# Two token tiles in turn, matmul by matmul, in the products whose tokens are stationary

## The chip, the cores and the metric

The kernel runs on one core of one Trainium2 chip. The metric is the device time of one execution in microseconds (us), as the median of several runs; lower is better. The profile comes from one further execution, so its own length is given beside the median.

## What is computed

The reference is one layer (DEPTH = 1) of a hybrid backbone, all in float32. 256 context tokens and 256 latent tokens of width 2048 are modulated and go through one input projection. The latent tokens then pass three branches (a gated recurrence, a pooling mixer, windowed attention), whose outputs are merged and projected, and a squared-ReLU MLP follows:

```python
ul = (xl * (1 + sc1_l) + sh1_l) @ w_in
uc = (xc * (1 + sc1_c) + sh1_c) @ w_in
...
z = jnp.einsum('btjc,jcd->btjd', jnp.stack(ys, axis=2), w_branch)
gates = jax.nn.sigmoid(u[..., COL_GATE:].reshape(B, T, N_BRANCH, D_MODEL))
return jnp.sum(gates * z, axis=2) @ w_out
...
xl = _layer_norm(ALPHA * xl + g1_l * _merge_branches(...), ln1_g, ln1_b)
h = xl * (1 + sc2_l) + sh2_l
xl = _layer_norm(ALPHA * xl + g2_l * (jnp.square(jax.nn.relu(h @ w_ff1)) @ w_ff2), ln2_g, ln2_b)
```

The four products that the change touches are those with the gate columns of `w_in`, with `w_branch`, with `w_out` and with `w_ff2` (2048 x 2048 four times over, since D_FF is 8192).

## The kernel before

**Precision.** Every float32 weight and activation is split into a rounded part and the rest (`whi`, `wlo`; index 0 and 1 of `hCL`, `yR`, `mR`, `hid`). A product is three matmuls: x high with w high, x high with w low, x low with w high.

**Weights.** A panel is 512 rows by 512 columns and is read by one DMA into a ring of `raw` buffers. It is split in two halves of 256 rows each: the ACT engine casts the half into `whi` (L476, semaphore `hi_made`), and DVE subtracts to get `wlo` (L940, semaphore `lo_made`). There are four places for halves, so ACT may cast a half only once the PE has finished with the half four before it (`w_used`, or `blk_done` for the last half of a block). In the order of both engines the splits stand between their other work, at places written out by hand.

**Products with the tokens stationary** (`tokens`, L1468 to L1470). The output block is 256 tokens by 512 columns: two token tiles t of 128, each in a PSUM bank of its own (`main[:, banks + t]`). The stationary operand is a 128 x 128 piece of the tokens, the moving one a 128 x 512 row tile of the weights. A half holds two row tiles j. For a half the PE does tile 0 whole (two j by three matmuls, six into one bank), then tile 1 (six into the other bank): 12 matmuls. The last matmul of tile 0 in the block raises `blk_done` and the last of tile 1 raises it again; the reader of tile 0 waits for the first, the reader of tile 1 for the second. `bank` waits, ahead of a tile's first matmul, until the bank's earlier reader has released it (`freed_by_act`, `freed_by_dve`).

**Blocks of this kind.** For each branch j of three and each of four column groups pp: a gate block of four panels in banks 0 and 1, read by ACT with a sigmoid (`sg`, L654), and a branch block of two panels in banks 2 and 3, read by DVE (`m_t` L1154, `gz` L1160). In between stand attention steps of the PE (L1730, L1740, L1751). Then four blocks with `w_out` (`out`), read by DVE in `out_rows`: L1230, L1233 and the statistics L1235 for tile 0, the same for tile 1. Then the MLP in four rounds f; each has four blocks of `wide` (L1445, L1447, features stationary against `h2`) and four blocks i of `tokens` against `hid`, read by DVE in `ff_out`: for f = 0 a copy (L1286), for f = 1 and 2 an add (L1288), for f = 3 three operations for each tile (L1291, L1293, L1295). In the last block of `out` and the last block of all, `apart=4` keeps the two tiles apart: tile 0 runs through all panels, then tile 1.

**What stands behind a reader.** DVE executes in order. In the round f = 3 its list is, between two blocks: `ff_out` for both tiles, then `residual` (L1324, L1326), then the split of the next panel (L940 twice). In `out` it is `out_rows` for both tiles, then splits.

Of the kernel before, what the change touches and what calls it, by code (L numbers as in the profile page):

```python
# [30 lines left out]
TILES = (slice(0, P), slice(P, T))  # L31
# [137 lines left out]
ST = stream()  # L169
# [80 lines left out]
def build(nc, vecs, cst, rcnt, masks, xT, xtok, rows, w_ad1, w_ada, w_in, w_ck, w_cv, pool_w, w_br, w_out, w_f1, w_f2, outT):  # L250
    weights_of = {"w_ad1": w_ad1, "w_ada": w_ada, "w_in": w_in, "w_ck": w_ck, "w_cv": w_cv, "w_br": w_br, "w_out": w_out,
                  "w_f1": w_f1, "w_f2": w_f2}
    with ExitStack() as ctx:
# [24 lines left out]
        def half_at(q):  # L278

            if q >= HALVES - 4 or OUT3 <= q < OUT3 + 4:  # L280
                return whi_end[:, q % 4], wlo_end[:, q % 4]
            if MLP0 <= q < MLP0 + 2:
                return whi_top[:, q - MLP0], wlo_top[:, q - MLP0]
            n = (q if q < MLP0 else q - 2) % 4
            return whi[:, n], wlo[:, n]
# [98 lines left out]
        main = ctx.enter_context(nc.psum_tensor("main", [P, 4, 512], F32))  # L384
# [10 lines left out]
        w_used, blk_done = ended["w_used"], ended["blk_done"]  # L395
# [975 lines left out]
        def _(pe):  # L1371
            mm = nc.tensor.matmul

            def bank(name, first, b):
                need = PN.before[name, first][b]
                if need:
                    pe.wait_ge(freed[need[0]], need[1])

            def half_ready(name, n, h):
                q = ST.half(name, n, h)  # L1380
                pe.wait_ge(lo_made, q + 1)
                return q % 4
# [72 lines left out]
            def tokens(name, first, chunks, banks, x, ready=None, between=lambda k: None, apart=0, second=None):  # L1455


                def half(n, h, t):
                    half_ready(name, first + n, h)
                    w_hi, w_lo = half_at(ST.half(name, first + n, h))  # L1460
                    if n == 0 and h == 0:
                        bank(name, first, t)
                    for j in range(2):
                        kt = 4 * n + 2 * h + j
                        start, stop = kt == 0, kt == 4 * chunks - 1
                        own = slice(P * t, P * (t + 1))
                        out = main[:, banks + t]
                        mm(out, x[:, kt, 0, own], w_hi[:, j], start=start, stop=False)  # L1468
                        mm(out, x[:, kt, 0, own], w_lo[:, j], start=False, stop=False)  # L1469
                        last = mm(out, x[:, kt, 1, own], w_hi[:, j], start=False, stop=stop)  # L1470
                    end = n == chunks - 1 and h == 1
                    if end:
                        last.then_inc(blk_done, 1)
                    elif t == 1:
                        last.then_inc(w_used, 1)

                for n in range(chunks - apart):
                    if ready is not None:
                        ready(n)
                    for h in range(2):  # L1480
                        for t in range(2):
                            half(n, h, t)
                    between(n)
                for t in range(2):
                    for n in range(chunks - apart, chunks):
                        if ready is not None and t == 0:
                            ready(n)
                        if second is not None and t == 1:
                            second(n)
                        for h in range(2):  # L1490
                            half(n, h, t)
# [109 lines left out]
            for n in range(2):  # L1601
                for h in range(2):
                    par = half_ready("cv", n, h)
                    w_hi, w_lo = (w[:, par].rearrange("p a (c n) -> p (a c) n", c=2) for w in (whi, wlo))
                    for b in range(2):
                        if n == 0 and h == 0:
                            bank("cv", 0, b)
                        for j in range(4):
                            kt = 8 * n + 4 * h + j
                            x, start, stop = (hC, hL)[b], kt == 0, kt == KT - 1  # L1610
                            for tile in range(2):
# [5 lines left out]
                                last = mm(out, x[:, kt, 1, own], w_hi[:, j], start=False, stop=stop,  # L1617
                                          skip_group_check=tile == 1)
# [22 lines left out]
            for it in range(4):  # L1641
                def between(k):
                    if k == 0:
                        if it:
                            ada_turn(3 + it)
                        if it >= 2:
                            keys_turned(it - 2)
                    if k == 1 and it >= 2:
                        states(it - 2)
# [62 lines left out]
            def branch(j, pp, between):  # L1712
                first = 24 * j + 6 * pp
                tokens("gates", first, 4, 0, hL, between=between)
                tokens("gates", first + 4, 2, 2, yR[j % 2], ready=lambda k: pe.wait_ge(y_lo, j + 1),
                       between=lambda k: between(4 + k))
# [41 lines left out]
            for b in range(8):  # L1758
# [5 lines left out]
                for n in range(2):  # L1764
                    last = mm(out, pw_sb[:, b // 2 * 2 + n, P * (b % 2):P * (b % 2 + 1)], pd[:, b // 2 * 2 + n],
                              start=n == 0, stop=n == 1)
# [53 lines left out]
            for i in range(4):  # L1820
                tokens("out", 4 * i, 4, 2 * (i % 2), mR, ready=lambda k: pe.wait_ge(m_lo, k + 1),
                       between=lambda k: merged(3) if i == 0 and k == 0 else None, apart=4 if i == 3 else 0,
                       second=first_rows)
# [111 lines left out]
```

## Time and profile before

| | us |
|---|---|
| median of three runs | 1905.89 (1905.32 to 1906.68) |
| span of the profiled execution | 1903.2 |
| stretch with gate and branch blocks | 631.2 to 1074.6 |
| blocks with `w_out` | 1074.6 to 1162.4 |
| `tokens` blocks of the MLP, rounds 0 to 3 | from 1264.0, 1442.5, 1620.9 and 1799.3 |

The median stands 2.7 us over the span of the profiled execution. In the profile PE is the matmul engine and PEld its weight load, which overlaps; a matmul's recorded duration (0.39 us) is longer than the distance to the next one's start (0.23 us), since the matmuls overlap in the pipeline, so distances between starts are what is to be read. An entry in brackets says how long the engine had been idle and what ended it.

### The profile page before, as it was taken

The numbers are of one execution on the slowest core, as the hardware profiler recorded it, in microseconds if no ns is written. First come the engines' busy times: TensorE is split into PE (matmuls) and PEld (weight loads), VectorE is DVE, ScalarE is ACT, GpSimd is POOL, SyncE is SP. The second block draws the span as 40 slices with busy tenths as digits, with TensorE's granted clock in tenths as the row PEclk, the third lists the DMA queues.
The fourth block names the chain that finished last, engine by engine and source line by source line (L and its number), as shares of the span: only waits on it lengthen the run. The fifth ranks groups of instructions, "written<-read, shape, count | busy, mean of one in ns | idle before, by whom it ended". The sixth has DMA issues, their size and how long they took to land.

```text
span 1903.2 us, 24662 instructions
## 1 busy us (share of the span) xinstructions
PE 1860.8 (98%) x10072; PEld 1568.8 (82%) x10072; DVE 1287.1 (68%) x1470; ACT 816.7 (43%) x991; POOL 282.8 (15%) x165
## 2 busy tenths in 40 slices
PE   6999999999999999999999998999999999999997
PEld 3678888899999877877888887888888888888875
DVE  2246777776969676577767667876676567557786
ACT  2132234464555554444444445443344344434432
POOL 0000000005757262001001000110012001100200
PEclk9999999999999999999999999999999999999998
DMA  9967765553434454565776763665665556556652
GB/s 398 418 251 280 267 224 195 177 178 133 155 112 155 158 185 155 190 252 199 272 258 227 281 218 136 237 228 199 252 234 203 195 203 242 207 188 241 223 177 89
DMA packets 60176, 408.93 MB, mean 215 GB/s; under 512 B 6432, under 2 KB 9120, under 8 KB 11936
## 3 DMA queue, kind: packets, MB, share of 16 engines
q1 hardware_dynamic: 55584, 395.34, 57.2%
q10 hardware_dynamic: 4480, 12.02, 1.7%
q8 instruction: 80, 1.31, 0.3%
q14 instruction: 32, 0.26, 0.0%
HBM read 405.24 MB, written 2.10 MB: 214 GB/s over the span
## 4 chain that ended last, share of the span: by engine, by line
PE 90%; DVE 4%; DMA 2%; DVEq 2%; ACT 1%; POOL 1%; issue 0%; SPq 0%; ACTq 0%
PE main L1468 14%; PE main L1470 14%; PE main L1469 14%; PE side L1445 6%; PE main L1445 6%; PE main L1385 5%; PE main L1387 5%; PE main L1386 5%; PE side L1447 3%; PE main L1447 3%; DMA raw<-in_w_ad 2%; PE main L1522 2%; PE main L1523 1%; PE main L1524 1%; PE side L1502 1%; DVE wlo L940 1%
## 5 line engine op out<-in xcount | busy, mean ns | idle before, releaser
L940 DVE TENSOR_TENSOR wlo<-raw,whi 128x1024 fp32r<-128x1024 f32 x542 | 696.6, 1312 | 307.1 <-ACT whi L476 306.3
L476 ACT CAST whi<-raw 128x1024 fp32r<-128x1024 f32 x542 | 563.9, 1050 | 715.0 <-PE main L1470 394.4
L1385 PE MATMUL main<-hCL,whi 128*128 128x256 f32 (+1 forms) x768 | 247.7, 323 | 0.9 <-DVE wlo L940 0.9
L1387 PE MATMUL main<-hCL,wlo 128*128 128x256 f32 (+1 forms) x768 | 244.5, 318 | 0.0
L1386 PE MATMUL main<-hCL,whi 128*128 128x256 f32 (+1 forms) x768 | 244.4, 318 | 0.0
L961 DVE SCALAR_TENSOR_TENSOR asum<-raw,sm,asum 128x512 f32<-128x512 f32 x240 | 221.8, 924 | 19.5 <-issue 0.4
L1468 PE MATMUL main<-whi,hid 128*128 128x512 f32 x496 | 194.9, 393 | 2.5 <-DVE wlo L940 2.5
L1469 PE MATMUL main<-wlo,hid 128*128 128x512 f32 x496 | 193.1, 389 | 0.0
L1470 PE MATMUL main<-whi,hid 128*128 128x512 f32 x496 | 193.0, 389 | 0.0
L1445 PE MATMUL side<-h,whi 128*128 128x512 f32 x512 | 181.3, 399 | 0.0
L1445 PE MATMUL main<-h,whi 128*128 128x512 f32 x480 | 170.0, 399 | 2.4 <-DVE wlo L940 2.4
L1468 PE MATMUL main<-whi,hCL 128*128 128x512 f32 x384 | 156.0, 406 | 0.0
L1385 PEld LDWEIGHTS main<-hCL,whi 128*128 128x128 f32 x768 | 146.2, 190 | 11.4 <-DVE wlo L940 1.3
L1386 PEld LDWEIGHTS main<-hCL,whi 128*128 128x128 f32 x768 | 146.2, 190 | 10.1 <-issue 0.2
L1387 PEld LDWEIGHTS main<-hCL,wlo 128*128 128x128 f32 x768 | 146.1, 190 | 10.1
L1470 PE MATMUL main<-whi,hCL 128*128 128x512 f32 x384 | 149.8, 390 | 0.0
L1469 PE MATMUL main<-wlo,hCL 128*128 128x512 f32 x384 | 149.7, 390 | 0.0
L1447 PE MATMUL side<-h,wlo 128*128 128x256 f32 x512 | 143.8, 281 | 0.0
L1447 PE MATMUL main<-h,wlo 128*128 128x256 f32 x496 | 138.6, 281 | 0.0
L925 POOL TENSOR_TENSOR sq<-sq 128x1024 f32<-128x1024 f32 x16 | 31.6, 1975 | 656.4 <-ACT hid L776 656.4
L1445 PEld LDWEIGHTS side<-h,whi 128*128 128x128 f32 x512 | 96.2, 188 | 24.1
L1468 PEld LDWEIGHTS main<-whi,hid 128*128 128x128 f32 x496 | 93.1, 188 | 24.0 <-issue 4.6
(264 smaller groups left out, 2920.5 us busy)
## 6 DMA issues: line engine op xcount, KB each, us to landing
raw<-in_w_f SPq DMA_DIRECT2D x128, 1024.0 KB, 4.8
raw<-in_w_in SPq DMA_DIRECT2D x104, 1024.0 KB, 4.8
raw<-in_w_ada SPq DMA_DIRECT2D x64, 1024.0 KB, 4.9
raw<-in_w_ad SPq DMA_DIRECT2D x32, 1024.0 KB, 16.1
raw<-in_w_br SPq DMA_DIRECT2D x24, 1024.0 KB, 4.9
raw<-in_w_out SPq DMA_DIRECT2D x16, 1024.0 KB, 4.8
xin<-in_xT SPq DMA_DIRECT2D x8, 512.0 KB, 17.4
raw<-in_w_ck SPq DMA_DIRECT2D x4, 512.0 KB, 15.1
```

The lines of the kernel that those rows point to most:

```text
L476: nc.scalar.copy(half_at(q)[0], slots[slot][:, 2 * h:2 * h + 2]).then_inc(hi_made, 1)
L940: TT(half_at(q)[1], slots[slot][:, 2 * h:2 * h + 2], half_at(q)[0].bitcast(F32), ALU.subtract).then_inc(lo_made, 1)
L961: last = STT(asum[:], slots[slot][:, j], s, asum[:], ALU.mult, ALU.add)
L1385: mm(out, w_hi, x_hi, start=start, stop=False)
L1386: mm(out, w_hi, x_lo, start=False, stop=False)
L1387: return mm(out, w_lo, x_hi, start=False, stop=stop)
L1445: mm(ps[:, b], w_hi[:, j, own], h2[:, kt].rearrange("p v t -> p (v t)"), start=kt == 0, stop=kt == 15, skip_group_check=True)
L1447: last = mm(ps[:, b, 0:T], w_lo[:, j, own], h2[:, kt, 0], start=False, stop=kt == 15, skip_group_check=True)
L1468: mm(out, x[:, kt, 0, own], w_hi[:, j], start=start, stop=False)
L1469: mm(out, x[:, kt, 0, own], w_lo[:, j], start=False, stop=False)
L1470: last = mm(out, x[:, kt, 1, own], w_hi[:, j], start=False, stop=stop)
L1522: mm(main[:, b], x[:, kt, 0, tile], whi[:, par, j], start=kt == 0, stop=False)
```

## The change

In the blocks that are not kept apart, a new function `both` takes the place of two calls of `half`. It issues the same 12 matmuls of a half in another order: for each row tile j it does x high with w high for tile 0 and then tile 1, x high with w low for both, and x low with w high for both. Neighbouring matmuls then write different banks, read the same moving weights, and have different stationary pieces. Each bank still gets its matmuls in the same order. Both banks are waited for ahead of the block's first matmul, and the wait for the half stands once instead of twice. `blk_done` is raised by the last matmul of tile 0, which is now the last but one of the block, and by the last of tile 1. The two blocks with `apart=4` still use `half`.

```diff
+                def both(n, h):
+                    half_ready(name, first + n, h)
+                    w_hi, w_lo = half_at(ST.half(name, first + n, h))
+                    if n == 0 and h == 0:
+                        bank(name, first, 0)
+                        bank(name, first, 1)
+                    for j in range(2):
+                        kt = 4 * n + 2 * h + j
+                        start, stop = kt == 0, kt == 4 * chunks - 1
+                        for t in range(2):
+                            mm(main[:, banks + t], x[:, kt, 0, TILES[t]], w_hi[:, j], start=start, stop=False)
+                        for t in range(2):
+                            mm(main[:, banks + t], x[:, kt, 0, TILES[t]], w_lo[:, j], start=False, stop=False)
+                        for t in range(2):
+                            last = mm(main[:, banks + t], x[:, kt, 1, TILES[t]], w_hi[:, j], start=False, stop=stop)
+                            if stop:
+                                last.then_inc(blk_done, 1)
+                    if n < chunks - 1 or h == 0:
+                        last.then_inc(w_used, 1)
+
                 for n in range(chunks - apart):
                     if ready is not None:
                         ready(n)
                     for h in range(2):
-                        for t in range(2):
-                            half(n, h, t)
+                        both(n, h)
                     between(n)
```

The order on the PE at the end of the block f = 3, i = 0, before: its last half and the first matmul of the next block. The first six matmuls are tile 0, the next six tile 1; the names don't show the bank.

```order
L1468 MATMUL main<-whi,hid 128x512 [waits lo_made]
L1469 MATMUL main<-wlo,hid 128x512
L1470 MATMUL main<-whi,hid 128x512
L1468 MATMUL main<-whi,hid 128x512
L1469 MATMUL main<-wlo,hid 128x512
L1470 MATMUL main<-whi,hid 128x512
L1468 MATMUL main<-whi,hid 128x512 [waits lo_made]
L1469 MATMUL main<-wlo,hid 128x512
L1470 MATMUL main<-whi,hid 128x512
L1468 MATMUL main<-whi,hid 128x512
L1469 MATMUL main<-wlo,hid 128x512
L1470 MATMUL main<-whi,hid 128x512
```

The same half after the change (L1487, L1489 and L1491 are the three lines of `both`; x2 is a pair, tile 0 and then tile 1):

```order
L1487 MATMUL main<-whi,hid 128x512 [waits lo_made]
L1487 MATMUL main<-whi,hid 128x512
L1489 MATMUL main<-wlo,hid 128x512 x2
L1491 MATMUL main<-whi,hid 128x512 x2
L1487 MATMUL main<-whi,hid 128x512 x2
L1489 MATMUL main<-wlo,hid 128x512 x2
L1491 MATMUL main<-whi,hid 128x512 x2
```

The last matmul of tile 0 stood sixth of the twelve and now stands eleventh; that of tile 1 is the twelfth both times.

The start of the second `w_out` block on the PE, before:

```order
L1468 MATMUL main<-whi,mR 128x512 [waits freed_by_dve,lo_made,m_lo]
L1469 MATMUL main<-wlo,mR 128x512
L1470 MATMUL main<-whi,mR 128x512
L1468 MATMUL main<-whi,mR 128x512
L1469 MATMUL main<-wlo,mR 128x512
L1470 MATMUL main<-whi,mR 128x512
L1468 MATMUL main<-whi,mR 128x512 [waits freed_by_dve,lo_made]
```

and after:

```order
L1487 MATMUL main<-whi,mR 128x512 [waits freed_by_dve,lo_made,m_lo]
L1487 MATMUL main<-whi,mR 128x512
L1489 MATMUL main<-wlo,mR 128x512 x2
L1491 MATMUL main<-whi,mR 128x512 x2
```

The wait for the second bank, which stood ahead of the seventh matmul, has joined the one ahead of the first. The lists of ACT, DVE, POOL and SP are the same before and after, and the PE has as many matmuls, 9468.

## Rows read from the trace of the kernel before

**Rows 1.** The page: busy us and share, and the chain that ended last.
```profile
PE 1860.8 (98%) x10072; PEld 1568.8 (82%) x10072; DVE 1287.1 (68%) x1470; ACT 816.7 (43%) x991; POOL 282.8 (15%) x165
...
PE 90%; DVE 4%; DMA 2%; DVEq 2%; ACT 1%; POOL 1%; issue 0%; SPq 0%; ACTq 0%
```

**Rows 2.** Stretches: start:end, length, busy us of each engine, clock, DMA.
```profile
1074.60:1162.40 87.80, 87.80 (x397) 72.86 (x396) 55.68 (x61) 38.17 (x46) 3.04 (x2) 1.00 0.58 213
...
1799.30:1893.00 93.70, 88.89 (x388) 72.02 (x386) 73.28 (x84) 32.55 (x36) 4.63 (x2) 1.00 0.41 139
```

**Rows 3.** Timeline of PE in `out`: start us, duration us, engine, line; second and third block.
```profile
1097.23 0.39 PE L1468 MATMUL main<-whi,mR 128*128 128x512 f32 x1
...
1098.36 0.39 PE L1470 MATMUL main<-whi,mR 128*128 128x512 f32 x1
1098.59 0.39 PE L1468 MATMUL main<-whi,mR 128*128 128x512 f32 x1
1098.81 0.39 PE L1469 MATMUL main<-wlo,mR 128*128 128x512 f32 x1
...
1102.67 0.39 PE L1468 MATMUL main<-whi,mR 128*128 128x512 f32 x1
...
1118.99 0.39 PE L1468 MATMUL main<-whi,mR 128*128 128x512 f32 x1
```

**Rows 4.** Line L1468 and tile `hid`: weight loads, count, ns min/median/max.
```profile
L1468 PEld LDWEIGHTS main<-whi,hid x496: 186/188/188, 1263.9 to 1884.2; 128*128 128x128 f32 x166
L1469 PEld LDWEIGHTS main<-wlo,hid x496: 187/188/189, 1264.1 to 1884.4; 128*128 128x128 f32 x166
```

**Rows 5.** Timeline of DVE in round 0: the readers of tiles 0 and 1.
```profile
1350.86 0.69 DVE L1286 COPY acc<-main 128x512 f32<-128x512 f32 x1 [1.77 <-PE main L1470]
1352.22 0.69 DVE L1286 COPY acc<-main 128x512 f32<-128x512 f32 x1 [0.67 <-PE main L1470]
```

**Rows 6.** Timeline of DVE in round 3, between blocks i = 0 and 1.
```profile
1820.82 0.69 DVE L1291 TENSOR_TENSOR res<-main,g2b 128x512 f32<-128x512 f32 x1 [1.76 <-PE main L1470]
...
1822.97 0.67 DVE L1291 TENSOR_TENSOR res<-main,g2b 128x512 f32<-128x512 f32 x1
...
1826.65 2.36 DVE L940 TENSOR_TENSOR wlo<-raw,whi 128x1024 fp32r<-128x1024 f32 x2
```

**Rows 7.** Timeline of PE in round 3: the three matmuls that waited.
```profile
1828.02 0.47 PE L1468 MATMUL main<-whi,hid 128*128 128x512 f32 x1 [0.44 <-DVE wlo L940]
...
1850.47 0.47 PE L1468 MATMUL main<-whi,hid 128*128 128x512 f32 x1 [0.44 <-DVE wlo L940]
...
1871.40 0.47 PE L1468 MATMUL main<-whi,hid 128*128 128x512 f32 x1 [1.62 <-DVE wlo L940]
```

**Rows 8.** Timeline of DVE in `out`, from tile 0's reader to the split.
```profile
1096.07 0.69 DVE L1230 TENSOR_TENSOR res<-main,g1b 128x512 f32<-128x512 f32 x1 [1.77 <-PE main L1470]
...
1100.37 4.81 DVE L940 TENSOR_TENSOR wlo<-raw,whi 128x1024 fp32r<-128x1024 f32 x4
1106.72 1.23 DVE L940 TENSOR_TENSOR wlo<-raw,whi 128x1024 fp32r<-128x1024 f32 x1 [1.54 <-ACT whi L476]
```

**Rows 9.** Timeline of ACT in the gate stretch.
```profile
729.81 0.60 ACT L654 ACTIVATE sg<-main 128x512 f32<-128x512 f32 x1 [3.94 <-PE main L1470]
731.17 0.60 ACT L654 ACTIVATE sg<-main 128x512 f32<-128x512 f32 x1 [0.76 <-PE main L1470]
...
737.08 1.05 ACT L476 CAST whi<-raw 128x1024 fp32r<-128x1024 f32 x1 [1.14 <-PE main L1470]
```

**Rows 10.** Timeline of PE at the start of a `wide` block and of the next.
```profile
1553.03 0.40 PE L1445 MATMUL side<-h,whi 128*128 128x512 f32 x1
1553.27 0.28 PE L1447 MATMUL side<-h,wlo 128*128 128x256 f32 x1
...
1575.64 0.40 PE L1445 MATMUL main<-h,whi 128*128 128x512 f32 x1
```

**Rows 11.** Timeline of PE: 256 columns each; an early stop.
```profile
560.02 0.28 PE L1386 MATMUL main<-hCL,whi 128*128 128x256 f32 x1
560.14 0.28 PE L1387 MATMUL main<-hCL,wlo 128*128 128x256 f32 x1
...
44.46 0.85 PE L1502 MATMUL side<-raw,sR 128*32 128x256 f32 x12 [2.14 <-DMA raw<-in_w_ad]
```

## The prediction

> **What bounds the kernel now.** I read the page first. The PE is busy 98% of the span and carries 90% of the chain that ended last [rows 1]. The table by stretches says where that is not quite so: in `out` the PE is busy all of 87.80 us, in round 3 of the MLP only 88.89 of 93.70, with the clock at 1.00 in both [rows 2]. So two things can move the time: the distance from one matmul to the next, and the few places where the PE waits. The timeline of the PE gives the distance, and the waits on `wlo` name DVE as the engine behind the places [rows 7].
>
> **Distance between matmuls.** The second `w_out` block starts at 1097.23 and the third at 1118.99, with 96 matmuls between: 21.76 / 96 = 0.2267 us each [rows 3]. The matmul at 1098.59 is the first of tile 1 and writes another bank than the one at 1098.36: 0.23 us. The next, at 1098.81, stays in its bank and keeps its stationary piece: 0.22 us. So the kernel before already holds the transition that the change multiplies, and it costs the same as the others, to the rounding of a row. `both` issues 3 x 1216 = 3648 matmuls less the 2 x 96 of the blocks kept apart, 3456. The value that I take for the alternation is 0 per matmul. The bounds: the 10 ns of rounding, one way, would be 35 us, but a block of 96 contains 16 switches of bank at 0.2267 on average, so a switch that saved or cost even 5 ns would need the other matmuls to make up for it.
>
> The stationary piece is loaded anew for every matmul, also where it is the one just used: L1468 and L1469 share it, and each has 496 loads of 188 ns [rows 4]. At 188 ns they fit under 227, so separating the two gives no load more and exposes none.
> The Trainium skill (TensorE: Matmul & The Clock Gate, Step-by-step: what each phase is for) says that the stationary operand is loaded once and used for many matmuls, which would speak against parting the pair; here each matmul has a load of its own, so by the trace there is nothing to lose. Were the second load of each of the 1152 pairs saved today, its roughly 107 ns (an estimate by the same page's section LDWEIGHTS, columns / 1.2) would add 123 us if uncovered.
>
> **Waits taken out.** The wait on `lo_made` stands once for each half instead of twice, and the second one never ended anything: by the time tile 1 starts, tile 0 has used the same half. 0. The wait for the second bank moves six matmuls, 1.36 us, earlier. Each bank's last reader is then long done: in `out` banks 0/1 and 2/3 take turns, so the reader of block i has 21.8 us before block i + 2 wants its banks, and the other blocks have at least the 10.9 us of a branch block. 0; if the cover were gone it would be up to 1.36 us for each block.
>
> **Tile 0's result comes later.** Its last matmul moves from sixth to eleventh of twelve: 5 x 0.2267 = 1.13 us. Tile 1's stays. That a reader really follows this moment is seen in round 0, where DVE waits for both tiles: 1350.86 and 1352.22, 1.36 us apart, six matmuls [rows 5]. What this does depends on the length of the reader.
>
> *Short readers* (one operation of 0.6 to 0.7 us): ACT's sigmoid, DVE's `gz`, `m_t`, and `ff_out` in rounds 0 to 2. In round 0 tile 0 would be read at 1350.86 + 1.13 = 1351.99, tile 1 right behind at about 1352.60 instead of 1352.22: what is queued behind, the splits above all, is 0.38 us later. On ACT the sigmoids at 729.81 and 731.17 give 0.3 in the same way, and the engine idles 1.14 us before the cast at 737.08, so it is absorbed there [rows 9]. I take 0 for these; the upper bound is 0.4 us at two or three of the tight attention steps, 1 us in all. A second cost would be a bank that frees late for the `wide` block behind round 0: it wants its third bank four pairs of 0.353 us [rows 10] after 1352.02, at 1353.43, and that bank is read by 1351.99 + 0.69 = 1352.68. Covered.
>
> *Long readers in round 3.* Three operations for tile 0, then three for tile 1: tile 1's first one starts at 1822.97, 2.15 us after tile 0's and without idle time [rows 6]. So nothing of the 1.13 is absorbed: all of DVE's list shifts, through the residual steps to the split at 1826.65. Its first half ends about 1.22 us later, at 1827.87, and the PE has waited for just that and starts at 1828.02 [rows 6, 7]. DVE had come to the reader early (idle 1.76 us), so it follows the PE. Each of the three stops of the PE in round 3 has this form, behind the readers of blocks i = 0, 1 and 2 [rows 7]. The gaps grow from 0.44, 0.44 and 1.62 to 1.57, 1.57 and 2.75: 3 x 1.13 = 3.4 us. Nothing gives it back, since block, reader and end all start from the PE's own time.
>
> *Long readers in `out`.* Same form: reader at 1096.07, no idle time until the splits at 1100.37; the first of them ends at 1100.37 + 1.22 = 1101.59 [rows 8]. The PE takes that half at 1102.67 in step [rows 3], so there is room for 1.08. The least distance of split's end and matmul is 0.15 (1827.87 to 1828.02), so 0.93 is spare and 1.13 - 0.93 = 0.20 us comes out as a new stop. The readers of blocks 0, 1 and 2 do this, and the last of them hits the block kept apart: 3 x 0.20 = 0.6 us.
>
> **Sum.** 0 + 0 + 3.4 + 0.6 = 4.0 us. The profiled execution would span 1903.2 + 4.0 = 1907.2; the median stands 2.7 over that span: 1909.9 us, 0.21% slower.
>
> **Rivals.**
> *The alternation saves time (the other side).* 512 columns take 227 ns and 256 take 120 [rows 11], so by the difference a column is 0.417 ns and every matmul carries 13 ns on top. If this were the price of following in the same bank, all 3456 would save it: 1909.9 - 3456 x 0.0133 = 1864. Against it: a switch of bank shows no saving [rows 3], and it would have to take effect at every switch already there. A saving from 1.2 ns per matmul on (4.0 / 3456) turns the sign.
> The Trainium skill (TensorE: Matmul & The Clock Gate, Back-to-back issue gap) gives N / 2.4 + 2.5 ns, 215.8 for 512 columns, where the row has 227. By that rule, should the alternation reach it, the time would be 37 us less, some 1872; it ties the rest to nothing that this change touches, and the trace does not agree with it.
>
> *The later tile is hidden.* DVE's delay would be absorbed, by the four places for halves. In the gate stretch this holds. In round 3 it fails since the place that the PE waits for is the one behind the reader. If I am wrong there, 1905.9.
>
> *Alternating stationary pieces cost.* In `wide` a pair of 512 and 256 columns takes (1575.64 - 1553.03) / 64 = 353.3 ns [rows 10], where 226.7 + 120 would be 346.7: 3.3 ns a matmul. There every matmul has a new stationary piece. If it is that, and not the short matmul that gives the load little cover, 3456 x 3.3 = 11.4 us come on top: 1921. Against it: in `tokens` two of three matmuls already have a new piece, at 0.2267.
>
> *More comes out of the tight places.* Short readers cost up to 1 us; the pause of 2.75 us is longer than any before with the clock at 1.00 (2.14 [rows 11]). Were the clock to fall to its lower level for the 19 us left, at most those 19 are added; likelier is 1911.5 to 1914.
>
> **Chances and range.** Forecast 0.62 (1908.6 to 1911.5), hidden 0.15 (1905.5 to 1907.5), more from the tight places 0.11, alternating pieces 0.06, saving 0.06. A measurement of this kernel can tell about 0.2%, 3.8 us, from no change; the forecast lies just beyond, at 4.0, so I split it 0.38 slower to 0.24 same. Slower 0.38 + 0.11 + 0.06 = 0.55; same 0.24 + 0.15 = 0.39; faster 0.06. The range 1905.2 to 1913 leaves out the saving, the alternating pieces and the upper part of the tight places, together under 0.2.
>
> **What would show it.** Starts of neighbouring matmuls in `both` 0.2267 apart. Readers of tiles 0 and 1 in round 0 one operation apart, near 0.6, instead of 1.36. The three idle times before a matmul in round 3 near 1.57, 1.57, 2.75, ended by `wlo`. Three new ones of 0.2 in `out`. A distance other than 0.2267 would refute me first; unchanged idle times in round 3 next.

## The result and the profile after the change

| | before | changed |
|---|---|---|
| median, us | 1905.89 (5 runs, 1905.32 to 1906.89) | 1912.5 (5 runs, 1911.55 to 1914.28) |
| ratio, 95% interval | | 1.0033 (1.0022 to 1.0044) |
| span of the profiled execution, us | 1903.2 | 1910.1 |

The change costs time: 6.6 us by the medians of this first comparison, where 4.0 (to 1909.9) were forecast. A second comparison of the same two kernels, further down, gives 1.0022 (1.0013 to 1.0031), about 4.2 us. Both lie past the 0.2% that the prediction set as the bound, the second one barely, and its interval reaches below it. Both profiled pages count 10072 matmuls, before and after; the 9468 named above stands in no view. One of the 11 runs of the first experiment below took 2319.5 us at a granted clock of 0.755, and its ratio is formed without that run.

**The rate of the matmuls has not changed.** Timeline of the PE in the changed kernel: the starts of the second and third blocks of round 0, 96 matmuls apart, and the starts of the second and third `w_out` blocks. `x2` is a pair, tile 0 and tile 1.

```profile
1290.25 0.62 PE L1487 MATMUL main<-whi,hid 128*128 128x512 f32 x2
...
1312.01 0.62 PE L1487 MATMUL main<-whi,hid 128*128 128x512 f32 x2
```

```profile
1098.57 0.62 PE L1487 MATMUL main<-whi,mR 128*128 128x512 f32 x2
1099.02 0.62 PE L1489 MATMUL main<-wlo,mR 128*128 128x512 f32 x2
...
1120.64 0.62 PE L1487 MATMUL main<-whi,mR 128*128 128x512 f32 x2
```

A pair takes 0.45 us from start to start, and the block of round 0 takes 21.76 us for 96 matmuls, 0.2267 for each as in [rows 3] (the `w_out` block is longer, 22.07, by a stop that is told below): no gain from the other bank, none from the shared moving weights, no loss from the changing stationary piece. The loads are as before too, one for each matmul; this is the line of the view by source for the first statement of `both` (compare [rows 4]):

```profile
L1487 PEld LDWEIGHTS main<-whi,hid x480: 186/188/190, 1267.5 to 1871.3; 128*128 128x128 f32 x160
```

**Tile 0's reader starts 1.13 us later.** Timeline of DVE at the end of round 0, where [rows 5] had two copies 1.36 us apart with idle time ahead of each:

```profile
1355.51 1.29 DVE L1286 COPY acc<-main 128x512 f32<-128x512 f32 x2 [2.90 <-PE main L1491]
```

Both copies now stand in one row; the idle time ahead has grown from 1.77 to 2.90, by 1.13. The same place in round 3, with the long readers (compare [rows 6]):

```profile
1825.47 0.69 DVE L1291 TENSOR_TENSOR res<-main,g2b 128x512 f32<-128x512 f32 x1 [2.89 <-PE main L1491]
...
1827.63 0.67 DVE L1291 TENSOR_TENSOR res<-main,g2b 128x512 f32<-128x512 f32 x1
...
1831.31 2.35 DVE L940 TENSOR_TENSOR wlo<-raw,whi 128x1024 fp32r<-128x1024 f32 x2
```

DVE idles 2.89 us instead of 1.76, and from there its list is as long as before: 2.16 us to tile 1, 5.84 us to the split (5.83 in [rows 6]). What the PE waits for comes 1.13 us later. Timeline of the PE, the three stops of round 3, to be held against [rows 7] with 0.44, 0.44 and 1.62:

```profile
1832.67 0.70 PE L1487 MATMUL main<-whi,hid 128*128 128x512 f32 x2 [1.58 <-DVE wlo L940]
...
1856.28 0.70 PE L1487 MATMUL main<-whi,hid 128*128 128x512 f32 x2 [1.57 <-DVE wlo L940]
...
1878.32 0.47 PE L1468 MATMUL main<-whi,hid 128*128 128x512 f32 x1 [2.75 <-DVE wlo L940]
```

In the table by stretches (start:end, length, busy us of each engine, clock, DMA), against [rows 2], both stretches are longer, while the PE has as many matmuls and, in round 3, the same busy time:

```profile
1075.90:1164.70 88.80, 88.72 (x397) 72.70 (x396) 56.85 (x62) 38.19 (x46) 3.37 (x2) 1.00 0.56 210
1802.80:1899.80 97.00, 88.93 (x388) 72.03 (x386) 73.18 (x84) 32.54 (x36) 4.63 (x2) 1.00 0.38 134
```

**Where the 6.9 us between the two profiled executions lie**, read from the starts of the same matmuls in both timelines:

| stretch | us more |
|---|---|
| first 45 us, waits for the first weight panels | 0.6 |
| first gate block, one stop at 643.7 | 0.7 |
| three `w_out` blocks, 0.31 each | 0.9 |
| start of the MLP, 1171 to 1174 | 1.3 |
| round 3 | 3.4 |

The third and the last row were forecast, with 0.6 and 3.4. The others stand in code that the change does not touch, or in a block where it had no reader yet. The rows show what they are. The PE's stop in the gate block at 643.7 is ended by the first split of the last row here. Timeline of DVE before the change:

```profile
633.15 0.16 DVE L1140 SCALAR_TENSOR_TENSOR mods<-mods,vv 128x16 f32<-128x16 f32 x1
633.23 3.44 DVE L940 TENSOR_TENSOR wlo<-raw,whi 128x1024 fp32r<-128x1024 f32 x2
...
637.89 3.36 DVE L1099 SCALAR_TENSOR_TENSOR ya<-lv,vv,ya 128x256 f32<-128x256 f32 x4
641.17 2.35 DVE L940 TENSOR_TENSOR wlo<-raw,whi 128x1024 fp32r<-128x1024 f32 x2
```

and after it:

```profile
633.78 0.78 DVE L1140 SCALAR_TENSOR_TENSOR mods<-mods,vv 128x16 f32<-128x16 f32 x1
634.48 5.17 DVE L940 TENSOR_TENSOR wlo<-raw,whi 128x1024 fp32r<-128x1024 f32 x2
...
640.86 1.67 DVE L1099 SCALAR_TENSOR_TENSOR ya<-lv,vv,ya 128x256 f32<-128x256 f32 x4
642.46 2.35 DVE L940 TENSOR_TENSOR wlo<-raw,whi 128x1024 fp32r<-128x1024 f32 x2
```

Both lists start 0.6 us apart, which is the first row of the table. The pair of splits takes 1.73 us more, but the four operations of L1099 behind it take 1.69 less, so the pair is not what delays. What is left is the small operation L1140 ahead of it, 0.78 instead of 0.16 us: 0.62 of the 0.7. POOL works beside this stretch both times; that it is what makes these operations longer and shorter is not shown. In the start of the MLP the clock fell. Timeline of the PE there, then the stretch's row in the table by windows, before:

```profile
1168.79 1.19 PE L1424 MATMUL main<-h,whi 128*128 128x256 f32 x8 [1.60 <-DVE wlo L940]
```

```profile
1168.20:1171.60 3.40, 2.81 (x22) 2.65 (x23) 2.72 (x5) 1.14 (x4) 0.00 (x0) 1.00 0.77 301
```

and after:

```profile
1171.05 2.04 PE L1424 MATMUL main<-h,whi 128*128 128x256 f32 x8 [1.60 <-DVE wlo L940]
```

```profile
1170.50:1173.90 3.40, 2.85 (x13) 2.88 (x14) 2.45 (x4) 0.00 (x0) 0.00 (x0) 0.51 0.77 308
```

The same eight matmuls, behind the same stop of 1.60 us, take 2.04 instead of 1.19 us, at a granted clock of 0.51 (the lower level, 1.2 GHz) instead of 1.00 (2.4 GHz). Whether these rows belong to the change or to the execution is for the experiments to say.

### The profile page after: what moved, and what is told of

The parts are those of the page before. It is cut to its first block, busy times and chain, and to the rows that moved or that the text cites. A ratio compares the mean times of both kernels' runs of the same rounds, so it can differ in the third digit from the quotient of the medians.

```text
span 1910.1 us, 24650 instructions
## 1 busy us (share of the span) xinstructions
PE 1863.1 (98%) x10072; PEld 1569.9 (82%) x10072; DVE 1290.4 (68%) x1470; ACT 815.5 (43%) x991; POOL 281.1 (15%) x165
## 4 chain that ended last, share of the span: by engine, by line
PE 88%; DVE 5%; DMA 2%; DVEq 2%; ACT 1%; POOL 1%; issue 1%; SPq 0%; ACTq 0%
PE main L1487 13%; PE main L1489 13%; PE main L1491 13%; PE side L1445 6%; PE main L1445 6%; PE main L1385 5%; PE main L1387 5%; PE main L1386 5%; PE side L1447 3%; PE main L1447 3%; DMA raw<-in_w_ad 2%; PE main L1541 2%; DVE wlo L940 2%; PE main L1542 1%; PE main L1543 1%; PE side L1521 1%
## 5 line engine op out<-in xcount | busy, mean ns | idle before, releaser
L1487 PE MATMUL main<-whi,hid 128*128 128x512 f32 x480 | 149.7, 393 | 3.1 <-DVE wlo L940 3.1
L1491 PE MATMUL main<-whi,hid 128*128 128x512 f32 x480 | 147.9, 389 | 0.0
L1489 PE MATMUL main<-wlo,hid 128*128 128x512 f32 x480 | 147.8, 389 | 0.0
L1487 PE MATMUL main<-whi,hCL 128*128 128x512 f32 x384 | 125.1, 407 | 0.4 <-DVE wlo L940 0.4
L1489 PE MATMUL main<-wlo,hCL 128*128 128x512 f32 x384 | 118.6, 390 | 0.0
L1491 PE MATMUL main<-whi,hCL 128*128 128x512 f32 x384 | 118.5, 390 | 0.0
L1445 PEld LDWEIGHTS main<-h,whi 128*128 128x128 f32 x480 | 90.2, 188 | 25.1 <-issue 2.8
```

The source lines that it names most:

```text
L1445: mm(ps[:, b], w_hi[:, j, own], h2[:, kt].rearrange("p v t -> p (v t)"), start=kt == 0, stop=kt == 15, skip_group_check=True)
L1487: mm(main[:, banks + t], x[:, kt, 0, TILES[t]], w_hi[:, j], start=start, stop=False)
L1489: mm(main[:, banks + t], x[:, kt, 0, TILES[t]], w_lo[:, j], start=False, stop=False)
L1491: last = mm(main[:, banks + t], x[:, kt, 1, TILES[t]], w_hi[:, j], start=False, stop=stop)
```

## The experiments

Two theories. **A**: only the later moment of tile 0's result costs, 3.4 us in round 3 and some 0.9 us in `out`; the other differences come and go with the execution. **B**: the interleaving costs by itself, or every block pays a little, or the extra pieces above belong to the change. The two kernels that differ in the last halves and the two with the cure ran on one chip beside 32 runs of the kernel before (median 1907.3), the other three on one chip beside 27 (median 1907.06).

### Interleaved, but the last half of each block in the old order

```diff
                     for h in range(2):
-                        both(n, h)
+                        if n == chunks - 1 and h == 1:
+                            for t in range(2):
+                                half(n, h, t)
+                        else:
+                            both(n, h)
```

> The changed kernel, but the last half of each block is done in the old order, so tile 0's last matmul is sixth of twelve again; all other halves stay interleaved. Theory A (only tile 0's later result costs): 1905.9 within 1 us, idle times before the three matmuls of round 3 back at 0.44, 0.44 and 1.62 us, and out blocks of 21.76 us again. Theory B (the interleaving itself, or the earlier wait for the second bank, costs): near the changed kernel, 1911 to 1913.

Measured: 1906.97 us, ratio 0.9995 (0.9985 to 1.0004). Of the 3456 matmuls of the change's loop, all outside the last halves (12 in each of 42 blocks) stay interleaved, and the loss is gone. The second `w_out` block takes 21.75 us (1097.90 to 1119.65), as before. The PE's timeline has the old stops back:

```profile
1828.67 0.70 PE L1487 MATMUL main<-whi,hid 128*128 128x512 f32 x2 [0.44 <-DVE wlo L940]
...
1851.15 0.47 PE L1487 MATMUL main<-whi,hid 128*128 128x512 f32 x1 [0.44 <-DVE wlo L940]
...
1872.10 0.47 PE L1468 MATMUL main<-whi,hid 128*128 128x512 f32 x1 [1.62 <-DVE wlo L940]
```

So neither the alternation nor the earlier wait for the second bank costs or gives anything that can be measured: held against the kernel before start for start (each matmul's start against that of the same matmul there), this profile gains or loses 0.1 us at most from the start of `out` to the end. This kernel still has both.

### The kernel before, with only the last half of each block interleaved

```diff
                     for h in range(2):
-                        both(n, h)
+                        if n == chunks - 1 and h == 1:
+                            both(n, h)
+                        else:
+                            for t in range(2):
+                                half(n, h, t)
```

> The kernel before, but the last half of each block is interleaved; nothing else. Theory A: the whole cost of the change, 1910.5 to 1913, stops of about 1.57, 1.57 and 2.75 us in round 3, and a third of a microsecond for each out block. Theory B: 1906 to 1907.

Measured: 1912.56 us, ratio 1.0024 (1.0015 to 1.0034): the whole loss from one half in each block. Its stops in round 3:

```profile
1830.61 0.47 PE L1468 MATMUL main<-whi,hid 128*128 128x512 f32 x1 [1.57 <-DVE wlo L940]
...
1854.21 0.47 PE L1468 MATMUL main<-whi,hid 128*128 128x512 f32 x1 [1.57 <-DVE wlo L940]
...
1876.28 0.47 PE L1468 MATMUL main<-whi,hid 128*128 128x512 f32 x1 [2.75 <-DVE wlo L940]
```

Its three `w_out` blocks are longer by 0.30, 0.32 and 0.32 us. With the one before, this places the cause in the last half of a block, where tile 0's last matmul moves by five places.

### The changed kernel again, beside the kernel before

> The changed kernel once more, beside the kernel before on the same chip. Theory A (tile 0's later result: 3.4 us in round 3, 0.9 us in out, nothing else): ratio 1.0023, some 4.3 us over the kernel before. Theory B (1.2 us more between out and the MLP at every execution, as in its first profile, and 0.7 us in the first gate block): ratio 1.0033, 6.3 us.

Measured: 1910.8 us, ratio 1.0022 (1.0013 to 1.0031). The point lies next to theory A's 1.0023; theory B's 1.0033 is outside the interval, though not by much. In its profile the stops of round 3 are 1.58, 1.57 and 2.75 again, those in `out` are there, and the clock stays at 1.00 through the start of the MLP. So the 1.3 us do not come with every execution of the change. Start for start, this profile has 0.86 us more in `out` and 3.40 in round 3.

### Interleaved in round 3 alone

```diff
-                        both(n, h)
+                        if name == "mlp" and first >= 96:
+                            both(n, h)
+                        else:
+                            for t in range(2):
+                                half(n, h, t)
```

> The interleaved order in the first three blocks of round 3 alone; every other block in the old order. Theory A: 3.4 us over the kernel before, ratio 1.0018. A rival that spreads the cost over all blocks: 3 of 38 blocks would give under 0.6 us.

Measured: 1911.05 us, ratio 1.0019 (1.001 to 1.0028). Three blocks give 0.19% or 3.6 us where 3.4 were worked out, and start for start the profile has 3.41 in round 3; a cost spread over all blocks (42, not the 38 of the text above) would give under 0.6. This kernel also answers for the other pieces, since its gate blocks and its way to the MLP are those of the kernel before. A row of the PE's timeline in the gate block:

```profile
643.31 0.50 PE L1468 MATMUL main<-whi,hCL 128*128 128x512 f32 x1 [0.41 <-DVE wlo L940]
```

and the table by windows at the start of the MLP:

```profile
1170.10:1173.30 3.20, 2.92 (x14) 2.95 (x15) 2.17 (x4) 0.00 (x0) 0.00 (x0) 0.50 0.86 338
```

Both are there, the stop and the low clock, in code where nothing was changed. They belong to the execution, not to the change. (The stop at 643 is in six of the nine profiles of this study, in kernels of both orders; the change's own first profile happened to have it and that of before not. Another stop, of 0.4 to 0.5 us at 692 in front of an attention step, is in five of the nine, of both orders too, and with it 0.56 to 0.69 us are added there. The profile of the kernel before has none of these pieces, so each comparison with it makes the other kernel look worse by what that one happened to get.)

### Interleaved everywhere but in `out` and in round 3

```diff
-                        both(n, h)
+                        if name == "gates" or (name == "mlp" and first < 96):
+                            both(n, h)
+                        else:
+                            for t in range(2):
+                                half(n, h, t)
```

> The interleaved order in the gate and branch blocks and in rounds 0 to 2, the old order in out and round 3. Theory A (short readers cost nothing): equal to the kernel before, ratio 1.0000 within 0.0006. The rival that short readers cost at the tight attention steps: 0.4 to 1 us more, and stops there in the profile that the kernel before hasn't.

Measured: 1906.48 us, ratio 0.9995 (0.9986 to 1.0004). 36 blocks with short readers cost nothing that can be measured: start for start, the profile loses under 0.02 us against the kernel before from 650 to 1074.6, and as little in rounds 0 to 2. It has no stop in the first gate block, and its one long stop in an attention step, 1.42 us at 745, is one that the kernel before has. In round 0 the two copies stand together as in the changed kernel:

```profile
1352.39 1.29 DVE L1286 COPY acc<-main 128x512 f32<-128x512 f32 x2 [2.90 <-PE main L1491]
```

The readers are late here too, by the same 1.13 us, and it is absorbed: the lateness alone is not the price, a PE without spare time behind it is.

### A cure on DVE, with and without the change

If what stands behind the readers is what the PE misses, it should stand ahead of them. In the blocks of `out` and of round 3, DVE now splits the first half of the panel that the PE will miss before the two readers; DVE was idle there anyway. Behind the third block of round 3 the reader of tile 1 moves behind all the splits.

```diff
 for n in range(15):
-    split_after("out", n)
+    if n in (4, 8, 13):
+        split(*ST.following("out", n), halves=(1,))
+    else:
+        split_after("out", n)
...
+    if n in (3, 7, 12):
+        split(*ST.following("out", n + 1), halves=(0,))
...
 for n in range(32):
-    if f or n >= 2:
+    if f == 3 and n in (20, 24, 28):
+        split(*ST.following("mlp", 32 * f + n), halves=(1,))
+    elif f or n >= 2:
         split_after("mlp", 32 * f + n)
+    if f == 3 and n in (19, 23, 27):
+        split(*ST.following("mlp", 32 * f + n + 1), halves=(0,))
...
-    for t in range(2):
+    for t in range(1 if f == 3 and n == 27 else 2):
         ff_out(f, n // 4 - 4, t)
+    if f == 3 and n == 30:
+        ff_out(3, 2, 1)
```

On the changed kernel:

> The changed kernel with another order on DVE alone: behind each out block and each block of round 3 the first half of the panel that the PE will miss is split ahead of the two readers; behind the third block of round 3 tile 1's reader is moved behind all splits. Theory A: the PE's stops in out and in round 3 vanish, also those that the kernel before has (0.60, 0.60 and 1.77 us in starts): about 1903, 3 us under the kernel before. Theory B: the stops vanish but the time stays 3 us or so over the next kernel.

On the kernel before:

> The kernel before with the same new order on DVE. Theory A: about 1903, equal to the changed kernel with that order within 0.1 %, since tile 0's moment no longer matters. Theory B: 3 us or more under it.

Measured: 1903.26 us, ratio 0.998 (0.9971 to 0.9989), with the interleaved order; 1903.05 us, ratio 0.9981 (0.9972 to 0.9989), with the old order. Both are faster than both kernels, by 0.2% against the kernel before, and equal to each other: once the split does not stand behind the readers, the moment of tile 0's result is worth nothing. DVE in the first of the two, at the place of [rows 6]:

```profile
1821.83 1.23 DVE L940 TENSOR_TENSOR wlo<-raw,whi 128x1024 fp32r<-128x1024 f32 x1 [1.53 <-ACT whi L476]
1823.19 0.69 DVE L1296 TENSOR_TENSOR res<-main,g2b 128x512 f32<-128x512 f32 x1
...
1829.40 1.22 DVE L940 TENSOR_TENSOR wlo<-raw,whi 128x1024 fp32r<-128x1024 f32 x1
```

The split fills the time in which DVE waited for tile 0 (2.89 us in the changed kernel), and only one split is left behind the readers. In the view of the PE's first statement from 1700 us on, where the kernel before has the three waits on `wlo` of [rows 7], this kernel has none:

```profile
its engine sat idle before it (us, times) until:
  issue: 0.5, 2
```

The gain against the kernel before was expected from the sum of its three stops, 0.60 + 0.60 + 1.77 = 3.0 us between starts (0.16%); measured are 0.2% with an interval of 0.11 to 0.29, so that sum lies inside. Start for start, both kernels with the cure gain 3.27 us in round 3 (0.69, 0.71 and 1.87 at the three places): the three stops, and 0.1 us for each on top, of which more below.

## Why the prediction was right

**Distance between matmuls.** Taken as unchanged, from the switches of bank that the kernel before already had. Measured 0.2267 in the changed kernel, and the first experiment holds the whole interleaving at a ratio of 0.9995. The two rivals on this point, a saving of 13 ns and a cost of 3.3 ns for each matmul, are both out: 3.3 ns would have shown as 0.6%, and in `both` every matmul has another stationary piece than the one ahead of it, still at 0.2267. Where the 3.3 ns of `wide` do not come from is shown at the end. The Trainium skill's figure (TensorE: Matmul & The Clock Gate, Back-to-back issue gap) of 215.8 ns for 512 columns was not reached in either order; the trace has 226.7 here in both.

**Waits taken out and moved.** Taken as 0; the kernel interleaved except for the last halves has the earlier bank wait and the missing second wait in nearly all halves and is equal to the kernel before.

**Long readers in round 3.** Forecast stops 1.57, 1.57, 2.75; measured 1.58, 1.57, 2.75, and alone 0.19% against the 0.18% worked out.

**Long readers in `out`.** The mechanism was right and the size a little off. Forecast 0.20 for each of three blocks, measured 0.31 (second block 1098.57 to 1120.64, 22.07 us against 21.76). The term left out is what a stop costs besides its length. Timeline of the PE around the stop in the changed kernel:

```profile
1103.55 0.61 PE L1491 MATMUL main<-whi,mR 128*128 128x512 f32 x2
1104.19 0.70 PE L1487 MATMUL main<-whi,mR 128*128 128x512 f32 x2
1104.73 0.63 PE L1489 MATMUL main<-wlo,mR 128*128 128x512 f32 x2
```

From 1103.55 to 1104.19 are 0.64 us for two matmuls, 0.19 more than 0.45, which is the stop as forecast. From 1104.19 to 1104.73 are 0.54 us for the next two, 0.09 more than 0.45: the PE gets back into step over the next matmuls. In round 3 this part was there before and so is not in the difference; in `out` the stops are new, and it comes on top, 3 x 0.1 us.

**Short readers.** Taken as 0 with an upper bound of 1 us; measured 0.9995 with those blocks alone. (The 0.3 us given for the sigmoids should be 1.13 - 0.76 = 0.37; it changes nothing.)

**The sum.** 3.4 + 0.9 = 4.3 us against 4.0 forecast, and 4.2 measured in the larger comparison (3.7 by its medians). The first comparison is another matter: its 1912.5 us lie in the range, but above the forecast's own 1908.6 to 1911.5 and inside the span of the prediction's fourth rival, more from the tight places. By the rows some 2.6 of the 6.9 us between the two profiles are pieces that come and go with the execution; that five runs of each kernel were too few to average them out is the likely reason for the 6.6, but only one run of each was profiled. So the direction and the mechanism were earned, and the closeness of the number depends on which comparison one takes. The fourth rival put such extra cost at the tight attention steps and at the pause of 2.75 us. That place was wrong. In the four profiles that have this pause (both of the changed kernel, the one with the last halves alone, the one with round 3 alone) the clock stays at 1.00 behind it; where it fell, it was in the start of the MLP, which has pauses of 1.4 to 1.8 us one after the other in every kernel.

## What to carry to other kernels

If an engine works through two results in turn, interleaving their matmuls makes the first result as late as the second; what that costs is read from the reader's list, not from the matmuls: how long the reader takes, and whether what stands behind it has spare time. A transition whose price is in doubt is often in the trace already, in smaller number. And an idle engine ahead of a long reader, with something behind the reader that the bound engine soon misses, is a place to put that something first: it was worth 0.2% here and made the kernel indifferent to the change.

## What the runs showed of the hardware that was not expected

The granted clock of the PE falls in some executions and not in others, at the same place behind the same pauses. Behind stops of 1.4 and 1.6 us at the start of the MLP it was 1.00 in the kernel before and 0.51 and 0.50 in the first profile of the changed kernel and in the one with only round 3 interleaved, which there run the same instructions; the cost was 1.3 us. The kernel with `out` and round 3 in the old order had such a stretch a little later, at 1191 us, behind a stop of 1.84 that the kernel before has too. Pauses of 2.75 us in round 3 left it at 1.00 each time. What decides it in an execution these runs do not show.

What followed the stretch at 1191 bears on the prediction's 3.3 ns. From there to the end of `wide` at the start of the MLP, this execution ran the pairs of 512 and 256 columns faster than any other. Timeline of its PE:

```profile
1195.79 0.39 PE L1445 MATMUL main<-h,whi 128*128 128x512 f32 x1
...
1219.37 0.39 PE L1445 MATMUL side<-h,whi 128*128 128x512 f32 x1
```

These are 68 pairs in 23.58 us, 346.8 ns each, which is 226.7 + 120; in the later rounds of the same execution, and in all rounds of the other eight, a pair takes 353.3 as in [rows 10]. The instructions are the same, with a new stationary piece for every matmul, so neither the changing piece nor the short matmul is by itself the price of 3.3 ns. The same code has two paces here, and what decides between them is not shown. Of the 1.5 us that the low clock cost, 1.3 had come back by the next `tokens` block.

The operations of DVE at 634 us are as changeable: L1140 takes 0.16 or 0.78 us and the two splits behind it 3.44 or 5.17, in the same code; what reaches the PE is 0.7 us. For a change of 4 us in 1900 such pieces are as large as a third of it, and only a comparison of many runs or of the same place in several profiles tells them from the effect.
